# The ends of five stages of a two-layer decoder trunk: unit 18's second token half later, the last three products behind the next transposes

## The chip, the cores and the metric

The kernel runs on one core of a Trainium2 chip. The metric is the device time of one execution in microseconds (us). The core's engines work from queues of their own and meet only at semaphores: TensorE (PE in the rows, its weight loads PEld), VectorE (DVE), ScalarE (ACT), GpSimd (POOL) and SyncE (SP), which issues most of the DMAs.

## What is computed

256 tokens of 1024 channels go through two layers. Each is a SwiGLU block, a token mixer and a second SwiGLU block, every one of them followed by a residual sum and a layer norm. The mixer is a causal pooling in the first layer and attention over a window of 128 in the second.

```python
def post_norm(x, sub, g, b):
    return layer_norm(DEEPNORM_ALPHA * x + sub, g, b)

def swiglu(x, w_gate, w_up, w_down):
    h = jax.nn.silu(x @ w_gate) * (x @ w_up)
    return h @ w_down

# in each layer
x = post_norm(x, 0.5 * swiglu(x, ffn_w_gate[i, 0], ffn_w_up[i, 0], ffn_w_down[i, 0]), ln_g[i, 0], ln_b[i, 0])
x = post_norm(x, mix, ln_g[i, 1], ln_b[i, 1])
x = post_norm(x, 0.5 * swiglu(x, ffn_w_gate[i, 1], ffn_w_up[i, 1], ffn_w_down[i, 1]), ln_g[i, 2], ln_b[i, 2])
```

The feed-forward width is 2816, in 22 units of 128. All is float32 in and out.

## The kernel before

**Numbers.** A product is made in a reduced float format (fp32r) from split operands: high part times high part, high times low, low times high. `three` issues these as three matmuls. ScalarE makes the high part of a weight (L545 for gate and up weights `g_hi`, L553 for down weights `d_hi`), VectorE the low part (L847 `g_lo`, L851 `d_lo`); one half unit of gate-up weights per stage is left to GpSimd (L384).

**Stages.** There are four feed-forward stages, f = 0 to 3. Pooling stands between 0 and 1, attention between 2 and 3. A stage has units u = 0 to 21. `gate_up(f, u)` computes gate and up of a unit. ScalarE applies silu (L562), VectorE multiplies (L862, `h_of`), ScalarE takes the high part (L572, `h_hi_of`), VectorE the low part (L867, `h_lo_of`). `ffn_down(f, u, ts, hs)` adds the unit to the output sums in PSUM, which are four banks: token half t = 0, 1 and channel half h = 0, 1. Each bank and unit costs one `three` of 512 columns. The waits for a unit's data stand at its products for t = 0.

**The end of a stage on TensorE.** After `gate_up(21)`, which is L1209 to L1211 with 256 columns, come 39 matmuls of 512 columns: unit 19, t 0, h 1 (3); unit 18, t 1 (6); units 20 and 21, t 0, h 0 and then h 1 (12); units 19, 20 and 21, t 1, h 0 and then h 1 (18). Then the next stage begins: `transposes(e, 0)` (L1311) brings the normed tokens of half 0 to channel-major form, four tiles for each of two channel halves q, `gate_up_tokens(f, 0)` (L1244, L1245, L1249) multiplies them with units 0 and 1, and `transposes(e, 1)` takes token half 1.

**The layer norm** is VectorE's. For t = 0 and then 1 it does residual sum and statistics for both channel halves (L929, L935), L939, L940, centring (L947) and scaling (L960). The power -0.5 is GpSimd's (L451). L929 waits for the semaphore `acc_done`, which the last product into each bank raises. The transposes wait for L960. ScalarE copies what they give (L624), and the token products wait for that copy.

**Splits for the next stage.** `g_split(f, u)` on ScalarE and VectorE makes high and low parts of a unit's gate-up weights, in two halves. On ScalarE the first half waits for the weights' DMA and for a count in `g_used`, which TensorE raises after the last product of a unit's gate and up:

```python
                    else:
                        after(act, g_used, G0[f] + (-1, 0, 0, 2)[u] if u < 4 else G - 1 + 4 * it)
```

`G0[f]` is the number of units ahead of stage f; for the attention's weights, f = None, the same table has 0 for u = 1 on top of `G_QKV`, the number of units ahead of attention. `silu_of(f, 21)` waits for `g_used` at `G0[f] + 22`. `next_first(f, 1)` is unit 1 of what follows stage f. Its first half is VectorE's, its second GpSimd's, for f = 1 and 2.

## Time and profile before

| | |
|---|---|
| median of 3 runs | 866.58 us (865.11 to 866.79) |
| the profiled execution, its own time | 865.43 us |
| its span, first to last instruction | 863.6 us |
| granted TensorE clock, mean | 0.997 |
| TensorE busy | 841.8 us, 97% of the span |
| VectorE busy | 566.5 us |
| ScalarE busy | 419.1 us |

A matmul's row shows its whole passage, and the next starts before it ends. So what one costs in a row of many is the distance between starts: 39 matmuls between 389.23 and the start of the transposes at 398.11 stand 0.227 us apart. The profiled execution's own time is 1.8 us longer than its span, for what lies around it.

### The profile page before, as it was taken

The page shows a single profiled execution, that of the slowest core. Times are in us where ns is not written, and L with a number is a line of the kernel's source. Part 1 is how long each engine was busy: PE and PEld are TensorE (multiplying, and loading weights), DVE is VectorE, ACT ScalarE, POOL GpSimd, SP SyncE. Part 2 cuts the span into 40 slices and gives each one's busy share as a digit, 9 for nine tenths or more (in the row PEclk, how much of TensorE's full clock was granted, in tenths as well). Part 3 has the DMA queues.
Part 4 walks back from the last instruction along what each step waited for, and adds up shares of the span by engine and source line. Part 5 has one row for each costly group of instructions (what it writes and reads, how often), then busy time and mean ns, then how long its engine had stood idle before and what let it go on. Part 6 is the DMA issues. An engine that isn't in the chain of part 4 may idle for free.

```text
span 863.6 us, 12144 instructions
## 1 busy us (share of the span) xinstructions
PE 841.8 (97%) x4484; PEld 712.5 (83%) x4484; DVE 566.5 (66%) x775; ACT 419.1 (49%) x651; POOL 51.3 (6%) x61
## 2 busy tenths in 40 slices
PE   7999999999999999999999999999998999999995
PEld 6888888878888888887888888887765888888885
DVE  2785565669846565668666565679889855655656
ACT  2555454552535455454445454454665544554540
POOL 0050000024000000002000000010002000000000
PEclk9999999999999999999999999999999999999998
DMA  9997556292755655556556546453517575465501
GB/s 280 348 327 248 167 186 201 92 292 91 249 192 188 200 189 194 173 184 222 201 167 222 178 163 220 173 192 122 171 33 250 184 240 188 155 226 168 188 0 49
DMA packets 116142, 162.17 MB, mean 188 GB/s; under 512 B 3936, under 2 KB 97632, under 8 KB 116112
## 3 DMA queue, kind: packets, MB, share of 16 engines
q1 hardware_dynamic: 112656, 152.06, 52.9%
q0 software_dynamic: 2496, 9.44, 3.2%
q8 instruction: 19, 0.31, 0.1%
q10 hardware_dynamic: 960, 0.27, 0.1%
q14 instruction: 11, 0.09, 0.0%
HBM read 160.70 MB, written 1.05 MB: 187 GB/s over the span
## 4 chain that ended last, share of the span: by engine, by line
PE 93%; DVE 4%; issue 1%; ACT 1%; DMA 1%; DVEq 0%; POOL 0%; SPq 0%
PE ps L1278 28%; PE ps L1276 16%; PE ps L1209 10%; PE ps L1210 10%; PE ps L1211 10%; PE ps L1275 4%; PE ps L1244 1%; PE ps L1245 1%; PE ps L1249 1%; PE ps L1229 1%; PE ps L1074 1%; PE ps L1077 1%; PE ps L1083 1%; PE ps L1311 1%; PE ps L1039 1%
## 5 line engine op out<-in xcount | busy, mean ns | idle before, releaser
L1278 PE MATMUL ps<-xT,g_hi 128*128 128x512 f32 x1064 | 379.3, 396 | 0.0
L1276 PE MATMUL ps<-xT,g_lo 128*128 128x256 f32 x1216 | 314.1, 279 | 0.0
L1276 PEld LDWEIGHTS ps<-xT,g_lo 128*128 128x128 f32 x1216 | 229.1, 188 | 12.5
L847 DVE TENSOR_TENSOR g_lo<-raw_g,g_hi 128x1024 fp32r<-128x1024 f32 x178 | 221.6, 1249 | 24.1 <-ACT g_hi L545 24.1
L1278 PEld LDWEIGHTS ps<-xT,g_hi 128*128 128x128 f32 x1064 | 199.7, 188 | 41.2
L857 DVE TENSOR_TENSOR gu<-ps,gu 128x512 f32<-128x512 f32 x76 | 52.5, 691 | 221.7 <-ACT gu L568 221.7
L545 ACT ACTIVATE g_hi<-raw_g 128x1024 fp32r<-128x1024 f32 x184 | 192.0, 1052 | 4.5 <-DMA raw_g<-in_ffn_w_up 2.9
L568 ACT ACTIVATE gu<-ps 128x512 f32<-128x512 f32 x76 | 45.6, 600 | 273.9 <-PE ps L1278 273.9
L1209 PE MATMUL ps<-d_hi,hT_hi 128*128 128x512 f32 x352 | 137.6, 391 | 2.1 <-DVE hT_lo L867 2.1
L1210 PE MATMUL ps<-d_lo,hT_hi 128*128 128x512 f32 x352 | 137.0, 389 | 0.0
L1211 PE MATMUL ps<-d_hi,hT_lo 128*128 128x512 f32 x352 | 136.9, 389 | 0.0
L851 DVE TENSOR_TENSOR d_lo<-raw_d,d_hi 128x1024 fp32r<-128x1024 f32 x96 | 117.3, 1224 | 5.0 <-ACT d_hi L553 5.0
L553 ACT ACTIVATE d_hi<-raw_d 128x1024 fp32r<-128x1024 f32 x96 | 99.9, 1047 | 3.1 <-DMA raw_d<-in_ffn_w_down 3.1
L1211 PEld LDWEIGHTS ps<-d_hi,hT_lo 128*128 128x128 f32 x352 | 66.1, 188 | 14.2
L1210 PEld LDWEIGHTS ps<-d_lo,hT_hi 128*128 128x128 f32 x352 | 66.1, 188 | 14.0
L1209 PEld LDWEIGHTS ps<-d_hi,hT_hi 128*128 128x128 f32 x352 | 66.1, 188 | 13.1 <-DVE hT_lo L867 2.4
L1275 PE MATMUL ps<-xT,g_hi 128*128 128x512 f32 x152 | 60.3, 396 | 0.0
L572 ACT ACTIVATE hT_hi<-hf_sink 128x256 fp32r<-128x256 f32 x82 | 34.3, 418 | 34.2 <-DVE hf_sink L862 33.8
L867 DVE TENSOR_TENSOR hT_lo<-hf_sink,hT_hi 128x256 fp32r<-128x256 f32 x82 | 36.5, 445 | 3.4 <-ACT hT_hi L572 3.4
L384 POOL TENSOR_TENSOR g_lo<-raw_g,g_hi 128x1024 fp32r<-128x1024 f32 x6 | 14.4, 2392 | 376.3 <-DVE g_lo L847 374.5
L562 ACT ACTIVATE gu<-gu 128x256 f32<-128x256 f32 x76 | 30.9, 407 | 5.7 <-DVE gu L857 5.7
L862 DVE TENSOR_TENSOR hf_sink<-gu 128x256 f32<-128x256 f32 x76 | 32.6, 429 | 1.0 <-ACT gu L562 1.0
(154 smaller groups left out, 684.6 us busy)
## 6 DMA issues: line engine op xcount, KB each, us to landing
raw_d<-in_ffn_w_down SPq DMA_DIRECT2D x87, 512.0 KB, 4.0
raw_g<-in_ffn_w_gate SPq DMA_DIRECT2D x43, 1024.0 KB, 5.5
raw_g<-in_ffn_w_up SPq DMA_DIRECT2D x43, 1024.0 KB, 7.9
raw_g<-in_attn_w_qkv SPq DMA_DIRECT2D x6, 1024.0 KB, 6.6
raw_d<-in_attn_w_o SPq DMA_DIRECT2D x8, 512.0 KB, 3.8
gb<-in_ln_g POOLq DMA_DIRECT2D x5, 512.0 KB, 4.0
gb<-in_ln_b POOLq DMA_DIRECT2D x4, 512.0 KB, 6.0
xn<-in_x SPq DMA_DIRECT2D x2, 512.0 KB, 6.1
```

The lines of the kernel that those rows point to most:

```text
L545: act.activation(g_half(g_hi, g_slot(f, u), half), src(G, half), ACT.Copy).then_inc(g_hi_done, 1)
L553: act.activation(d_hi[:, E % D_SLOTS, :], raw_d[:, (E // 2) % 2, E % 2, :], ACT.Copy).then_inc(d_hi_done, 1)
L568: act.activation(gu[:, u % 2, :, :], both[:, :, S:2 * S], ACT.Copy).then_inc(low_done, 1)
L847: dve.tensor_tensor(g_half(g_lo, g_slot(f, u), half), src(G, half), g_half(g_hi, g_slot(f, u), half).bitcast(f32), ALU.subtract).then_inc( ...
L851: dve.tensor_tensor(d_lo[:, E % D_SLOTS, :], raw_d[:, (E // 2) % 2, E % 2, :], d_hi[:, E % D_SLOTS, :].bitcast(f32), ALU.subtract).then_in ...
L857: dve.tensor_tensor(gu[:, u % 2, :, :], both[:, :, 0:S], gu[:, u % 2, :, :], ALU.add).then_inc(gu_done, 1)
L1209: pe.matmul(out_, l_hi, r_hi, start=start, stop=False)
L1210: pe.matmul(out_, l_hi, r_lo, start=False, stop=False)
L1211: return pe.matmul(out_, l_lo, r_hi, start=False, stop=stop)
L1275: pe.matmul(bank, w_hi, xT[:, k, :, :], start=True, stop=False)
L1276: last = pe.matmul(bank[:, S:2 * S], w_lo, xT_hi[:, k, :], start=False, stop=False)
L1278: last = pe.matmul(bank, w_hi, xT[:, k, :, :], start=False, stop=k == KT - 1)
```

## The change

In every stage, unit 18's two groups for t = 1 leave their place between unit 19 and unit 20 and are issued with the rest of t = 1. The last product of a stage, unit 21 into the bank t 1, h 1 (three matmuls), becomes `last_down`. It is issued behind `transposes(e, 0)` of what follows the stage; after stage 0 it stands behind the first `means` of pooling, and after stage 3 it stays at the end. The last product of attention's output, `wo` unit 7 into t 1, h 1, also goes behind the next transposes. A count that the transposes raised (`d_used`) is raised by a later matmul.

On ScalarE and VectorE the first half of `next_first(f, 1)`, for f = 1 and 2, is made at the end of unit 20 and no longer at the end of unit 21.

```diff
@@ ScalarE, unit(f, u)
                 if f == 0 and u == UNITS - 2:
                     g_split(1, 0)
+                if f in (1, 2) and u == UNITS - 2:
+                    g_split(*next_first(f, 1), halves=(0,))
                 if f < 3 and u == UNITS - 1:
-                    g_split(*next_first(f, 1))
+                    g_split(*next_first(f, 1), halves=(0, 1)[f > 0:])
@@ VectorE, unit(f, u)
-                if u == UNITS - 1:
-                    if f == 0:
-                        g_split(1, 0, halves=(1,))
-                    elif f < 3:
-                        g_split(*next_first(f, 1), halves=(0,))
+                if f == 0 and u == UNITS - 1:
+                    g_split(1, 0, halves=(1,))
+                elif f in (1, 2) and u == UNITS - 2:
+                    g_split(*next_first(f, 1), halves=(0,))
@@ TensorE, pooling
-                    if t == 0 and k == 0:
+                    if t == 1 and src == 0 and k == 0:
                         ins.then_inc(d_used, 1)
@@
             means(0, 0, 0, True, True)
+            last_down(0)
             means(1, 0, P, True, False)
@@ TensorE, attention
             transposes(e, 0)
+            last_down(2)
             qkv(0, 0, 0, part=0, d_counted=True)
@@
             for h in range(2):
-                for k in range(5, 8):
+                for k in range(5, 8 - h):
                     wo(k, (1,), hs=(h,))
@@ TensorE, gate_up_tokens
-                    pe.matmul(out_, xT_hi[:, k, tok], w_hi[:, :, :, k, :], start=k == 0, stop=False)
+                    ins = pe.matmul(out_, xT_hi[:, k, tok], w_hi[:, :, :, k, :], start=k == 0, stop=False)
+                    if f > 1 and t == 0 and k == 0:
+                        ins.then_inc(d_used, 1)
@@ TensorE, the stages
+            def last_down(f):
+                ffn_down(f, UNITS - 1, (1,), hs=(1,))
+
@@
-                transposes(e, 0, used=(0, 2, 1, 1)[f])
+                transposes(e, 0, used=(0, 2, 0, 0)[f])
+                if f == 2:
+                    last_down(1)
+                elif f == 3:
+                    down(D_WO + 7, xT_hi[:, 7, :], xT_lo[:, 7, :], (1,), False, True, hs=(1,))
@@
                 ffn_down(f, last_u + 1, (0,), hs=(1,))
-                ffn_down(f, last_u, (1,))
                 for h in range(2):
                     for u in (last_u + 2, last_u + 3):
                         ffn_down(f, u, (0,), hs=(h,))
                 for h in range(2):
-                    for u in range(last_u + 1, UNITS):
+                    for u in range(last_u, UNITS - h):
                         ffn_down(f, u, (1,), hs=(h,))
                 if f == 0:
-                    pool_pe(pe)
+                    pool_pe(pe, last_down)
                 if f == 2:
-                    attention_pe(pe, three, down, transposes)
+                    attention_pe(pe, three, down, transposes, last_down)
+                if f == 3:
+                    last_down(f)
```

Here `last_u` is 18. ScalarE at the end of stage 1, before: unit 20's last two instructions, unit 21 (silu and high part) and the two halves of the split for the next stage.

```order
L572 ACTIVATE hT_hi<-hf_sink 128x256 [waits hf_done]
L553 ACTIVATE d_hi<-raw_d 128x1024 [waits d_used,d_in0]
L562 ACTIVATE gu<-ps 128x256 [waits g_used]
L572 ACTIVATE hT_hi<-hf_sink 128x256 [waits hf_done]
L545 ACTIVATE g_hi<-raw_g 128x1024 [waits g_used,g_in0]
L545 ACTIVATE g_hi<-raw_g 128x1024
```

The same place after:

```order
L572 ACTIVATE hT_hi<-hf_sink 128x256 [waits hf_done]
L553 ACTIVATE d_hi<-raw_d 128x1024 [waits d_used,d_in0]
L545 ACTIVATE g_hi<-raw_g 128x1024 [waits g_used,g_in0]
L562 ACTIVATE gu<-ps 128x256 [waits g_used]
L572 ACTIVATE hT_hi<-hf_sink 128x256 [waits hf_done]
L545 ACTIVATE g_hi<-raw_g 128x1024
```

The first half's copy, with its wait for `g_used`, has moved from behind unit 21 to ahead of unit 21's silu.

VectorE at the same place, before: unit 20's low parts, unit 21's product and low part, the split's first half, the layer norm.

```order
L867 TENSOR_TENSOR hT_lo<-hf_sink,hT_hi 128x256 [waits h_hi_done]
L851 TENSOR_TENSOR d_lo<-raw_d,d_hi 128x1024 [waits d_hi_done]
L862 TENSOR_TENSOR hf_sink<-gu,ps 128x256 [waits silu_done]
L867 TENSOR_TENSOR hT_lo<-hf_sink,hT_hi 128x256 [waits h_hi_done]
L847 TENSOR_TENSOR g_lo<-raw_g,g_hi 128x1024 [waits g_hi_done]
L929 SCALAR_TENSOR_TENSOR xn<-ps,xn 128x512 [waits acc_done]
```

After (lines moved by one or two):

```order
L869 TENSOR_TENSOR hT_lo<-hf_sink,hT_hi 128x256 [waits h_hi_done]
L853 TENSOR_TENSOR d_lo<-raw_d,d_hi 128x1024 [waits d_hi_done]
L849 TENSOR_TENSOR g_lo<-raw_g,g_hi 128x1024 [waits g_hi_done]
L864 TENSOR_TENSOR hf_sink<-gu,ps 128x256 [waits silu_done]
L869 TENSOR_TENSOR hT_lo<-hf_sink,hT_hi 128x256 [waits h_hi_done]
L930 SCALAR_TENSOR_TENSOR xn<-ps,xn 128x512 [waits acc_done]
```

The split's low half now stands ahead of unit 21's product. TensorE behind stage 1, after: the transposes, `last_down(1)` and the first token products; before, L1311's rows were followed by L1244 at once.

```order
L1319 MATMUL ps<-cst,xn 128x128 [waits xn_done]
L1319 MATMUL ps<-cst,xn 128x128 x3
L1212 MATMUL ps<-d_hi,hT_hi 128x512
L1213 MATMUL ps<-d_lo,hT_hi 128x512
L1214 MATMUL ps<-d_hi,hT_lo 128x512
L1247 MATMUL ps<-g_hi,xT 128x512 [waits x_hi_done,g_lo_done]
L1250 MATMUL ps<-g_lo,xT 128x512
```

The three matmuls have come in between the transposes and the products that wait for ScalarE's copy.

## Rows read from the trace of the kernel before

**Rows 1.** The page, part 1: busy time, share, instructions of TensorE.
```profile
PE   841.8 (97%) x4484; PEld 712.5 (83%) x4484; DVE 566.5 (66%) x775; ACT 419.1 (49%) x651; POOL 51.3 (6%) x61
```
**Rows 2.** Timeline, ScalarE, end of stage 1: start, duration, line, operation, idle before.
```profile
389.43 0.38 ACT L562 ACTIVATE gu<-ps 128x256 f32<-128x256 f32 x1 [1.89 <-PE ps L1211]
...
390.63 1.99 ACT L545 ACTIVATE g_hi<-raw_g 128x1024 fp32r<-128x1024 f32 x2
```
**Rows 3.** Timeline, VectorE, end of stage 1.
```profile
389.85 0.42 DVE L862 TENSOR_TENSOR hf_sink<-gu,ps 128x256 f32<-128x256 f32 x1 [1.05 <-ACT gu L562]
390.75 0.42 DVE L867 TENSOR_TENSOR hT_lo<-hf_sink,hT_hi 128x256 fp32r<-128x256 f32 x1 [0.48 <-ACT hT_hi L572]
391.70 1.23 DVE L847 TENSOR_TENSOR g_lo<-raw_g,g_hi 128x1024 fp32r<-128x1024 f32 x1 [0.53 <-ACT g_hi L545]
392.86 0.69 DVE L929 SCALAR_TENSOR_TENSOR xn<-ps,xn 128x512 f32<-128x512 f32 x1
...
397.31 1.41 DVE L960 SCALAR_TENSOR_TENSOR xn<-xn,rstd,gb 128x512 f32<-128x512 f32 x2
...
399.96 0.67 DVE L929 SCALAR_TENSOR_TENSOR xn<-ps,xn 128x512 f32<-128x512 f32 x1
```
**Rows 4.** Timeline, TensorE, end of stage 1 and entry of stage 2.
```profile
389.23 0.40 PE L1209 MATMUL ps<-d_hi,hT_hi 128*128 128x512 f32 x1
...
397.87 0.39 PE L1211 MATMUL ps<-d_hi,hT_lo 128*128 128x512 f32 x1
398.11 1.32 PE L1311 MATMUL ps<-cst,xn 128*128 128x128 f32 x8
399.55 0.47 PE L1244 MATMUL ps<-g_hi,xT 128*128 128x512 f32 x1
...
406.40 0.50 PE L1244 MATMUL ps<-g_hi,xT 128*128 128x512 f32 x1
```
**Rows 5.** Timeline, TensorE, a wait in stage 0 and the matmuls behind it.
```profile
184.08 0.50 PE L1209 MATMUL ps<-d_hi,hT_hi 128*128 128x512 f32 x1 [2.12 <-DVE hT_lo L867]
184.42 0.40 PE L1210 MATMUL ps<-d_lo,hT_hi 128*128 128x512 f32 x1
```
**Rows 6.** Timeline, end of stage 0: that product, unit 21's low part, pooling's first matmuls.
```profile
190.63 0.40 PE L1209 MATMUL ps<-d_hi,hT_hi 128*128 128x512 f32 x1
...
192.15 0.42 DVE L867 TENSOR_TENSOR hT_lo<-hf_sink,hT_hi 128x256 fp32r<-128x256 f32 x1 [0.48 <-ACT hT_hi L572]
...
199.60 3.81 PE L1025 MATMUL ps<-qT,xn 128*128 128x128 f32 x32
```
**Rows 7.** Timeline, attention's end and entry of stage 3, TensorE.
```profile
668.62 1.32 PE L1311 MATMUL ps<-cst,xn 128*128 128x128 f32 x8 [1.99 <-DVE xn L960]
670.05 0.47 PE L1244 MATMUL ps<-g_hi,xT 128*128 128x512 f32 x1
```
**Rows 8.** Timeline, end of stage 3, TensorE and VectorE.
```profile
845.94 0.40 PE L1209 MATMUL ps<-d_hi,hT_hi 128*128 128x512 f32 x1
...
847.46 0.42 DVE L867 TENSOR_TENSOR hT_lo<-hf_sink,hT_hi 128x256 fp32r<-128x256 f32 x1 [0.48 <-ACT hT_hi L572]
...
849.57 0.69 DVE L929 SCALAR_TENSOR_TENSOR xn<-ps,xn 128x512 f32<-128x512 f32 x1 [1.68 <-PE ps L1211]
...
856.67 0.67 DVE L929 SCALAR_TENSOR_TENSOR xn<-ps,xn 128x512 f32<-128x512 f32 x1
```
**Rows 9.** Timeline, GpSimd and VectorE splits: one beside GpSimd in stage 0; GpSimd's in stage 1.
```profile
178.04 5.70 POOL L427 TENSOR_TENSOR raw_d<-raw_d,q_sb 128x1024 f32<-128x1024 f32 x2 [115.86 <-DMA raw_d<-in_pool_w]
178.10 3.44 DVE L847 TENSOR_TENSOR g_lo<-raw_g,g_hi 128x1024 fp32r<-128x1024 f32 x1
...
393.09 2.39 POOL L384 TENSOR_TENSOR g_lo<-raw_g,g_hi 128x1024 fp32r<-128x1024 f32 x1 [173.72 <-DVE g_lo L847]
```
**Rows 10.** Windows: stretch, length, busy times, PEclk (the granted clock), DMA share, GB/s.
```profile
180.00:190.00 10.00, 7.88 (x57) 7.21 (x57) 8.51 (x8) 4.28 (x6) 3.74 (x2) 1.00 1.03 325
...
855.00:863.60 8.60, 0.00 (x0) 0.00 (x0) 6.01 (x11) 0.00 (x0) 0.99 (x1) 0.74 0.33 122
```

More of the change, by code:

```diff
@@ L1015, in _, with pool_pe @@
                     layer_norm(5)
-        def pool_pe(pe):
+        def pool_pe(pe, last_down):
             def means(t, src, columns, first, last):
@@ L1050, in pool_pe, with attention_pe @@
             maps(1)
-        def attention_pe(pe, three, down, transposes):
+        def attention_pe(pe, three, down, transposes, last_down):
             ident = cst[:, 0, :]
```

## The prediction

> **What bounds the kernel now.** Read the engines' busy shares first: TensorE works in 97% of the span [rows 1]. So a matmul that is only moved costs and saves nothing by itself. What counts is the time in which TensorE has nothing to start, and the tail behind its last product, where VectorE's layer norm sets the end. Then read the timeline at each stage's end, by the distance between starts. From 389.23 to 398.11 stand 39 matmuls [rows 4]: 0.2275 us each, without a gap. Then come eight transposes. A pass of 128 columns takes 0.114 us (32 in 3.81 us, less 0.16 for the last one's passage) [rows 6], so eight are 0.91 us, but the token product starts 1.44 us behind the first of them [rows 4]. The missing 0.53 us are the second channel half's wait for VectorE and the token product's wait for ScalarE's copy. The first matmul behind a wait costs 0.11 us more than its place in a row: 0.34 us to the next start, from 184.08 to 184.42 [rows 5].
>
> Next, the norm at the end of stage 1. Unit 21's low part is finished at 390.75 + 0.42 = 391.17, 1.94 us behind 389.23, where `gate_up(21)` has ended for TensorE [rows 3, 4]. Stage 3 has 847.88 - 845.94 = 1.94 and stage 0 has 192.57 - 190.63 = 1.94 [rows 6, 8]. It is the bare chain of silu, product, high part and low part, the same at four stage ends. TensorE comes to unit 21 after 12 matmuls, 2.73 us, so 0.79 us of cover are left. That number decides what follows.
>
> **Unit 18 moved: all four stages.** Six matmuls go from ahead of unit 21 to behind it. TensorE comes there 1.36 us sooner, 1.37 us after `gate_up(21)`, and the chain needs 1.94. So unit 21's first product waits 0.58 us, 0.6 with the semaphore, plus 0.11 for the first matmul: a new stall of 0.7 us. The sums of token half 0, and with them the norm, come 2.73 - 1.94 - 0.15 = 0.65 us sooner.
>
> **Stage 3, the tail.** Its norm is not waited for by TensorE but is the end of the kernel. The first L929 goes from 849.57 to 848.9. The last bank is due at VectorE's fourth sum, at 856.67 before [rows 8] and 856.0 then. TensorE is done with it at 845.94 + 39 x 0.2275 + 0.16 + 0.7 = 855.7, still in time by 0.3 us. Gain: 0.65 us.
>
> **Stage 0.** Here the splits are not moved. The stall is +0.7. TensorE then waits for nothing else: pooling's first matmul stood at 199.60 [rows 6], 0.1 us behind the last product's slot. That 0.1 goes. The three last products move behind the first means and delay nothing but the second sums of the norm, which pooling needs only after its maps of token half 0. Cost: 0.6 us.
>
> **Stages 1 and 2, the split moved.** The wait it brings along is for `g_used` at G0[f+1] + 0, which is the count that TensorE raises behind `gate_up(21)` itself, the same that unit 21's silu waits for. ScalarE did sit idle 1.89 us ahead of that silu [rows 2], room for a copy, but the wait keeps it from using the room. The copy starts at 389.43 where the silu did. Queued behind it are the silu and everything of unit 21, and TensorE waits for these. A copy is 1.05 us in its queue (two in 1.99, overlapping by 0.1) [rows 2]. VectorE's low half starts at 390.52, takes 1.22 to 1.23 [rows 3], and stands ahead of `h_of(21)`, which starts at 391.66 and no longer at 389.85 [rows 3]: 1.81 us late. The low part of unit 21 ends at 392.98. TensorE came to it at 390.60 and waits until 393.02: 2.42 us, and 0.11 for the first matmul, 2.53 in all. Thirty matmuls remain ahead of the transposes (39 less 6 less 3): 393.13 + 6.82 = 399.95. VectorE's norm, 1.15 us later than before (L929 goes from 392.86 to 394.0, and the first half of L960 from 398.01 to 399.2) [rows 3], is ahead of that. So the transposes run without a wait to 400.86, the three last products fill to 401.54, and the token product starts there: 1.99 us after its old 399.55 [rows 4]. The copy that it needs is done at 401.1, hidden.
>
> The second sum of token half 1 now needs that last product: about 401.7, where VectorE took it up at 399.96 [rows 3], +1.75. TensorE is 1.99 - 0.11 later, so the norm of half 1 stays in step, and a remaining 0.1 us at the second transposes closes. Per stage +1.8 us at 406.40 [rows 4]. The end of stage 2 has the same pattern (39 matmuls, the same chain, the same transposes), so two times 1.8, 3.6 us. The half split itself is done earlier, and GpSimd's half (2.39 us) [rows 9] begins 0.5 us later, both off the path. The loads that SyncE issues behind it belong to units 4 and up, later in the stage.
>
> **The attention's last product moved.** TensorE waits there for the norm, 1.99 us [rows 7]. Three matmuls taken from before the wait only lengthen it, and put behind the transposes they take 0.68 us, of which the copy's wait hides 0.32 (the second four transposes start with the second half of L960, 0.66 us behind the first, and are done 1.11 us behind 668.62; the product starts 1.43 behind it [rows 7]) and the first-matmul cost another 0.11. Cost: 0.25 us. The idle there grows to 2.7 us.
>
> **Sum.** 0.6 + 1.8 + 1.8 + 0.25 - 0.65 = +3.8 us, on the profiled execution 865.43 + 3.8 = 869.2. The median of the runs is 866.58, 1.15 above it, so the forecast for a median is 870.4 us, slower by 0.44%. The terms' own bounds: each of the five stage-end costs may be off by 0.2 to 0.4 us (what a wait hides of the three matmuls), which makes +2.6 to +5.0.
>
> **A rule weighed.** VectorE's split took 3.44 us beside GpSimd's 5.70 us, and 1.23 elsewhere [rows 3, 9], so the two engines hold each other up. GpSimd's half split of stage 1 moves to about 393.6 to 396.0, and the centring L947, which reads two operands from SBUF, to 397.1: 1.1 us clear of it. The Trainium skill ("SBUF — State Buffer", "SBUF: two separate sides") says that the port pair of GpSimd and VectorE is an exclusive lock for a whole instruction, taken by a VectorE instruction with two SBUF inputs. By that rule an overlap would cost the rest of GpSimd's instruction, and none is expected here; the trace's 3.44 us agrees with a blocking, and no row tells how long a centring would be held.
>
> **Rivals.**
> (a) The wait is met early: some count makes `g_used` reach the value before `gate_up(21)` ends. Then copy and low half run in the idle 1.89 us, unit 21 is on time, and stages 1 and 2 pay what stage 0 pays, 0.7, less 0.53 and 0.1 of filled waits: +0.1 each. Sum 0.6 + 0.2 + 0.25 - 0.65 = +0.4, 867.0 us. For it speaks only the idle; against it stand the table and the place where TensorE raises the count. Chance 0.08.
> (b) Faster: unit 21 doesn't hold TensorE at all. It decides where the chain behind `gate_up(21)` falls from 1.94 to under 1.37 us. Then the moves only fill waits: stage 0 gains 0.1, stages 1 and 2 0.6 each, the tail 1.36, attention loses 0.25: -2.4, 864.2 us. Against it: 1.94 us at every stage end with ScalarE and VectorE idle before it, and the split added to it at two. Chance 0.03.
> (c) The granted clock falls in a new stall. It stayed at 1.00 through the wait of 2.12 us, and was 0.74 on average over the 8.6 us behind the last matmul [rows 5, 10], so it does fall in idleness. The new stalls of 2.4 and 2.7 us are a little longer than any that the trace shows clean. At 1.2 GHz for 2.4 each matmul of the 30 that follow would cost 0.23 us more, up to 6.8 us a stage: 873 to 884 us. Chance 0.03.
> (d) The norm of stages 1 and 2 runs into GpSimd's half split after all and is held up to 2.4 us; TensorE has 0.75 us of slack there (399.95 against 399.2), so up to +1.6 a stage, 872 to 873.6 us. Chance 0.03.
>
> **How the numbers follow.** The forecast has the remaining chance, 0.83. Its range, +2.6 to +5.0 on 866.58 and 0.7 us for how medians of one kernel scatter (865.11 to 866.79 in three runs), is 868.5 to 872.3; I take 868.2 to 872.2, which leaves out (a), (b), (c), most of (d) and little else, under 2 in 10. What a measurement can tell from no change is about 0.2%, 1.7 us. Slower by more: the forecast, (c) and (d), less 0.03 for a sum that comes out too small: 0.86. Within: (a) and that 0.03, with a rounding 0.11. Faster: (b), 0.03.
>
> **What would show it.** In the changed trace, ScalarE's g_hi copy starts right behind `gate_up(21)` at the ends of stages 1 and 2, and its silu 1 us later. TensorE has two waits of about 2.4 us for hT_lo there, and two of 0.6 us at the ends of stages 0 and 3. The transposes of stages 2 and attention show no wait for L960, attention's end one of 2.7 us. The tail behind the last matmul gets shorter by 1.3 us, from 8.6 to about 7.3. If the copy runs before the end of `gate_up(21)`, (a) holds and the time stays near 867. If the waits are there and the time isn't, the span is set by something that I read as hidden.

## The result and the profile after

The changed kernel takes 871.97 us at the median of 8 runs (868.88 to 873.95). The kernel before, run beside it, takes 865.36 us (864.78 to 866.79, 8 runs). The ratio is 1.007, with a 95% interval of 1.0056 to 1.0085: slower, by 6.6 us. The time lies inside the predicted range, 1.6 us above the forecast. Part of that is luck: the range was laid on a median of 866.58 us from three runs, and the same kernel's eight runs have 865.36. As a difference, +6.6 us lies above the forecast of +3.8 and its bounds of +2.6 to +5.0. The profiled execution took 870.46 us, +5.0 on the one of before.

The page's part 1, of after, answers to [rows 1]:

```profile
PE   842.6 (97%) x4484; PEld 714.9 (82%) x4484; DVE 566.9 (65%) x775; ACT 418.6 (48%) x651; POOL 51.5 (6%) x61
```

The work is the same: as many matmuls, 0.8 us more of passage. So the time lies in gaps. The waits of TensorE (us in total, times, longest us) name them:

```profile
PE ps L1212 <- DVE hT_lo L869: 6.9, 4, 2.3
...
PE ps L1319 <- DVE xn L961: 2.7, 1, 2.7
```

Before, the trace had one wait for hT_lo, 2.12 us, in stage 0 [rows 5], and one of 1.99 us for xn [rows 7]. Now there are four for hT_lo, one at each stage's end, and xn's has grown.

The end of stage 1 of after, in the timeline of ScalarE and VectorE, answers to [rows 2, 3]:

```profile
389.56 1.06 ACT L545 ACTIVATE g_hi<-raw_g 128x1024 fp32r<-128x1024 f32 x1 [1.95 <-PE ps L1214]
390.53 0.36 ACT L562 ACTIVATE gu<-ps 128x256 f32<-128x256 f32 x1
...
390.66 1.23 DVE L849 TENSOR_TENSOR g_lo<-raw_g,g_hi 128x1024 fp32r<-128x1024 f32 x1 [1.79 <-ACT g_hi L545]
391.80 0.41 DVE L864 TENSOR_TENSOR hf_sink<-gu,ps 128x256 f32<-128x256 f32 x1
...
392.69 0.43 DVE L869 TENSOR_TENSOR hT_lo<-hf_sink,hT_hi 128x256 fp32r<-128x256 f32 x1 [0.48 <-ACT hT_hi L572]
```

ScalarE's copy waits 1.95 us for TensorE and starts when `gate_up(21)` has ended. The silu stands behind it, and VectorE's low half of the split stands ahead of unit 21's product. TensorE in the same place, against [rows 4]:

```profile
389.30 0.40 PE L1212 MATMUL ps<-d_hi,hT_hi 128*128 128x512 f32 x1
...
393.17 0.50 PE L1212 MATMUL ps<-d_hi,hT_hi 128*128 128x512 f32 x1 [2.32 <-DVE hT_lo L869]
393.51 0.39 PE L1213 MATMUL ps<-d_lo,hT_hi 128*128 128x512 f32 x1
...
400.11 1.03 PE L1319 MATMUL ps<-cst,xn 128*128 128x128 f32 x8
400.90 0.47 PE L1212 MATMUL ps<-d_hi,hT_hi 128*128 128x512 f32 x1
...
408.41 0.50 PE L1247 MATMUL ps<-g_hi,xT 128*128 128x512 f32 x1
```

Unit 21's first product starts 3.87 us behind 389.30, after a wait of 2.32. The transposes have no wait, the last products follow them, and the second group of token products starts at 408.41, 2.01 us later than at 406.40.

Attention's end and the start of stage 3, of after, against [rows 7]:

```profile
672.55 1.97 PE L1319 MATMUL ps<-cst,xn 128*128 128x128 f32 x8 [2.67 <-DVE xn L961]
674.17 0.78 PE L1212 MATMUL ps<-d_hi,xT 128*128 128x512 f32 x1
674.74 0.63 PE L1213 MATMUL ps<-d_lo,xT 128*128 128x512 f32 x1
```

These rows are long. The last product's second matmul starts 0.57 us behind its first; in stage 1 the same step, from 400.90 to 401.22, took 0.32. The windows (length, busy us of PE, PEld, DVE, ACT and POOL with their counts, granted clock, DMA share, GB/s) say why:

```profile
670.00:675.00 5.00, 2.45 (x10) 2.36 (x11) 4.45 (x6) 1.04 (x2) 1.59 (x2) 0.73 0.62 198
675.00:680.00 5.00, 5.00 (x22) 4.03 (x22) 4.06 (x8) 2.05 (x3) 0.55 (x1) 0.93 0.71 225
```

The granted clock falls behind the wait of 2.67 us. The loss is (0.27 + 0.07) x 5 = 1.7 us of the full rate of 2.4 GHz, for a stretch of twice that at 1.2 GHz. Below this is called a low stretch; rival (c) named it.

The end of stage 3, of after, against [rows 8]:

```profile
851.74 0.38 ACT L562 ACTIVATE gu<-ps 128x256 f32<-128x256 f32 x1 [2.81 <-PE ps L1214]
...
853.54 0.50 PE L1212 MATMUL ps<-d_hi,hT_hi 128*128 128x512 f32 x1 [0.45 <-DVE hT_lo L869]
...
854.54 0.69 DVE L930 SCALAR_TENSOR_TENSOR xn<-ps,xn 128x512 f32<-128x512 f32 x1 [1.06 <-PE ps L1214]
...
860.92 0.39 PE L1214 MATMUL ps<-d_hi,hT_lo 128*128 128x512 f32 x1
```

Unit 21 waits 0.45 us. VectorE's idle ahead of its first residual sum has shrunk from 1.68 to 1.06 us. What each term of the sum measured is told behind the experiments.

### The profile page after: what moved, and what is told of

It reads as the page before. It is cut to its first block, busy times and chain, and to the rows that moved or that the text cites. A ratio compares the mean times of both kernels' runs of the same rounds, so it can differ in the third digit from the quotient of the medians.

```text
span 868.6 us, 12144 instructions
## 1 busy us (share of the span) xinstructions
PE 842.6 (97%) x4484; PEld 714.9 (82%) x4484; DVE 566.9 (65%) x775; ACT 418.6 (48%) x651; POOL 51.5 (6%) x61
## 4 chain that ended last, share of the span: by engine, by line
PE 91%; DVE 5%; ACT 2%; issue 1%; DMA 1%; DVEq 0%; POOL 0%; SPq 0%; ACTq 0%
PE ps L1283 28%; PE ps L1281 16%; PE ps L1212 10%; PE ps L1214 10%; PE ps L1213 10%; PE ps L1280 4%; PE ps L1247 1%; PE ps L1250 1%; PE ps L1254 1%; PE ps L1232 1%; PE ps L1076 1%; PE ps L1079 1%; PE ps L1085 1%; PE ps L1319 1%; DVE d_lo L853 1%
## 5 line engine op out<-in xcount | busy, mean ns | idle before, releaser
L853 DVE TENSOR_TENSOR d_lo<-raw_d,d_hi 128x1024 fp32r<-128x1024 f32 x96 | 119.5, 1247 | 5.2 <-ACT d_hi L553 5.2
```

Of the source, the lines that this page charges most:

```text
L853: dve.tensor_tensor(d_lo[:, E % D_SLOTS, :], raw_d[:, (E // 2) % 2, E % 2, :], d_hi[:, E % D_SLOTS, :].bitcast(f32), ALU.subtract).then_in ...
```

## The experiments

Two theories had to be told apart. **The wait theory** is the forecast's: what the change costs is the stall at unit 21, most of it because the moved copy waits for `g_used`. **The clock theory** is rival (c) in a small size: the new and longer waits let the granted clock fall in a part of the runs, and that explains the rest of the median and the spread of 5 us where the kernel before had 2. A third question was whether the parts are worth something without the faults. Each ratio below is against the kernel before, run beside the kernel on the same chip. Runs' mean clocks are given where they bear on it; they include the tail, in which TensorE has no work, so that 0.997 or more is a run without a low stretch. The fourteen profiled executions of this document bear that out: windows of 5 us show no low stretch in the six with 0.997 or more, one in the four with 0.995 or 0.996 (after, e6, e8, e9), two in the three with 0.993 or 0.994 (e1, e4, e5) and three in the one with 0.992 (e3), each a loss of 1.7 us of full rate.

### The split back (e1)

```diff
@@ after, ScalarE (and VectorE likewise)
-                if f in (1, 2) and u == UNITS - 2:
-                    g_split(*next_first(f, 1), halves=(0,))
                 if f < 3 and u == UNITS - 1:
-                    g_split(*next_first(f, 1), halves=(0, 1)[f > 0:])
+                    g_split(*next_first(f, 1))
```

> The changed kernel with one part undone: ScalarE and VectorE make the first half of the next stage's split at the end of unit 21 again; TensorE's order is the changed one. Theory (the split's wait for g_used costs 1.8 us at each of stages 1 and 2): +0.4 us over the kernel before, and TensorE's wait for hT_lo at those two ends is 0.6 us and not 2.3. Rival (TensorE's new order is what costs): the time stays near the changed kernel's, +4 us or more. Second theory (a stretch of about 3.4 us at 1.2 GHz, 1.7 us lost, follows the long idle ahead of stage 3, as in the profiled run of the changed kernel): up to +2.1 us where a run has it, since that idle of 2.7 us is still there.

Measured: 867.05 us, ratio 1.0016 (1.0007 to 1.0025, 11 runs). Without the split's move 1.5 of the 6.6 us are left. The eleven runs fall into two groups: 866.00 to 866.45 at a mean clock of 0.997 (five runs), and 867.98 to 868.55 at 0.993 to 0.996 (five), with one run between. So two things are at work, and the split is the larger. The profiled execution, 868.33 us, has two low stretches, behind a wait of 1.78 us in stage 0 and one of 2.67 us behind attention.

### The wait asked for earlier (e2)

The split stays where the change puts it, and its count in `g_used` is one that TensorE has long reached.

```diff
-                        after(act, g_used, G_QKV + (-1, 0, 0, 1, 3, 4)[u])
+                        after(act, g_used, G_QKV + (-1, -20, 0, 1, 3, 4)[u])
...
-                        after(act, g_used, G0[f] + (-1, 0, 0, 2)[u] if u < 4 else G - 1 + 4 * it)
+                        after(act, g_used, G0[f] + (-1, -20 if f < 3 else 0, 0, 2)[u] if u < 4 else G - 1 + 4 * it)
```

> The changed kernel with one number changed: the moved split waits for g_used at the value that unit 1 of the stage raises (the last reader of its slot), 20 lower, so the copy can run while gate_up(21) does. Theory (it was the wait and not the place): as the kernel with the split put back, +0.4 us over before, silu of unit 21 right behind gate_up(21), TensorE's wait for hT_lo 0.6 us at all four ends. Rival (two more instructions ahead of unit 21 cost by their work): +1.8 to +3.6 us. The clock stretch ahead of stage 3 may add 1.7 us in a run.

Measured: 867.16 us, ratio 1.0012 (1.0003 to 1.0021, 11 runs). Timeline of e2, end of stage 1:

```profile
388.03 1.04 ACT L545 ACTIVATE g_hi<-raw_g 128x1024 fp32r<-128x1024 f32 x1
390.03 0.38 ACT L562 ACTIVATE gu<-ps 128x256 f32<-128x256 f32 x1 [0.95 <-PE ps L1214]
...
391.83 0.50 PE L1212 MATMUL ps<-d_hi,hT_hi 128*128 128x512 f32 x1 [0.45 <-DVE hT_lo L869]
```

The copy now runs in ScalarE's idle time ahead of the silu, which is rival (a) made true by hand. Unit 21's wait is 0.45 us where it was 2.32. The instruction's place was harmless; the count that it waits for did the harm.

### The split alone (e4)

The kernel before with the split's move and nothing else.

```diff
@@ before, ScalarE (and VectorE likewise)
+                if f in (1, 2) and u == UNITS - 2:
+                    g_split(*next_first(f, 1), halves=(0,))
                 if f < 3 and u == UNITS - 1:
-                    g_split(*next_first(f, 1))
+                    g_split(*next_first(f, 1), halves=(0, 1)[f > 0:])
```

> The kernel before with only the split moved on ScalarE and VectorE (wait unchanged); TensorE's order is that of before. Theory: unit 21 is ready at 3.75 us behind gate_up(21) and TensorE comes to it at 2.73, so it waits 1.0 us, and the norm and all behind it come 1.1 us later at each of two stages: +2.2 us. Rival (the split's place is harmless while unit 18 stands ahead as cover): within 0.3 us of before.

Measured: 867.99 us, ratio 1.0020 (1.0011 to 1.0029, 11 runs), +2.4. Timeline of e4:

```profile
393.82 0.50 PE L1210 MATMUL ps<-d_hi,hT_hi 128*128 128x512 f32 x1 [0.96 <-DVE hT_lo L869]
```

With unit 18 still ahead of it TensorE has the 0.79 us of cover that the prediction counted, and waits 0.96 instead of 2.32. The split's move harms by itself, and unit 18's makes it worse by just the six matmuls (2.32 - 0.96 = 1.36 us). The wait is what the theory said. The median of +2.4 isn't free of the clock, though: the profiled execution, 869.97 us, has two low stretches, and the three runs at 0.997 or 0.998 took 865.59, 866.82 and 868.06.

### Attention's last product back (e3)

```diff
@@ after, attention and entry of stage 3
-                for k in range(5, 8 - h):
+                for k in range(5, 8):
...
-                elif f == 3:
-                    down(D_WO + 7, xT_hi[:, 7, :], xT_lo[:, 7, :], (1,), False, True, hs=(1,))
```

> The changed kernel with attention's last product put back ahead of the transposes; all else as changed. Arithmetic without a clock: 0.25 us less than the changed kernel, +3.5 over before, idle ahead of stage 3 2.0 us. Theory (the idle of 2.7 us there is what lets the clock fall): 1.5 to 2 us less than the changed kernel, and mean clock 0.997 as before. Rival (the waits of 2.3 us at the ends of stages 1 and 2 let it fall as well): the difference to the changed kernel stays under 1 us and runs at 0.993 to 0.995 remain.

Measured: 872.78 us, ratio 1.0073 (1.0059 to 1.0087, 5 runs), not below after. The clock theory in its first form said that the wait of 2.7 us behind attention is what lets the clock fall. It is 2.0 us here, and the low stretches are still there. Windows of e3:

```profile
185.00:190.00 5.00, 5.00 (x32) 5.00 (x32) 3.21 (x4) 3.66 (x5) 0.00 (x0) 0.71 0.87 271
...
585.00:590.00 5.00, 5.00 (x19) 4.03 (x18) 4.25 (x8) 0.00 (x0) 1.43 (x2) 0.77 0.62 200
...
675.00:680.00 5.00, 4.69 (x17) 3.72 (x18) 4.86 (x10) 3.09 (x4) 0.55 (x1) 0.66 1.03 340
```

And the waits of e3's TensorE, in its timeline:

```profile
183.27 0.50 PE L1212 MATMUL ps<-d_hi,hT_hi 128*128 128x512 f32 x1 [2.12 <-DVE hT_lo L869]
...
394.39 0.50 PE L1212 MATMUL ps<-d_hi,hT_hi 128*128 128x512 f32 x1 [2.32 <-DVE hT_lo L869]
...
582.52 0.50 PE L1212 MATMUL ps<-d_hi,hT_hi 128*128 128x512 f32 x1 [2.32 <-DVE hT_lo L869]
...
675.30 1.10 PE L1319 MATMUL ps<-cst,xn 128*128 128x128 f32 x5 [2.01 <-DVE xn L961]
```

Four waits of 2.0 to 2.3 us, and a low stretch behind three of them: behind 183.27, 582.52 and 675.30, not behind 394.39. The wait at 183.27 is the same 2.12 us behind which the clock stayed at 1.00 in the kernel before [rows 5, 10]. So waits of about 2 us let the clock fall at some times and not at others, and the first form of the theory is gone.

### Unit 18 alone (e5), the last products alone (e6)

```diff
@@ e5: before
-                ffn_down(f, last_u, (1,))
...
-                    for u in range(last_u + 1, UNITS):
+                    for u in range(last_u, UNITS):
@@ e6: before, stages 1 and 2 alone
-                    for u in range(last_u + 1, UNITS):
+                    for u in range(last_u + 1, UNITS - h * (f in (1, 2))):
```

e6 has `last_down(1)` and `last_down(2)` behind `transposes(e, 0)`, as the change has them.

> The kernel before with only unit 18's t = 1 products (six matmuls) issued with the rest of t = 1, in all four stages; last products, split and attention as before. Theory: unit 21 is reached 1.37 us behind gate_up(21) and ready at 1.94, so 0.7 us of stall at each of four stage ends; the norm comes 0.65 us sooner, which stages 0 to 2 can't use in full; the tail gives back 0.65. Stage 0 +0.6, stages 1 and 2 +0.3 to +0.5 each, stage 3 -0.65: +0.6 to +1.0 us. Rival (TensorE is free to start the norm sooner and the stage follows it): -0.6 us at each end, -2.5 us.

> The kernel before with only the last product of stages 1 and 2 issued behind the next transposes. Theory: the norm is ready at 398.06 in the time of the trace before, TensorE comes to the transposes at 397.43 and waits; then transposes and three matmuls end 1.8 us later, at 399.85 in place of 399.55: +0.2 us a stage, +0.4 in all. Rival (the three matmuls fill the copy's wait at no cost): 0 or -0.2 us a stage.

Measured: e5 867.26 us, ratio 1.0020 (1.0005 to 1.0034, 9 runs); e6 867.11 us, ratio 1.0016 (1.0004 to 1.0028, 9 runs). Neither part gains anything alone. Timeline of e5, then of e6:

```profile
392.87 0.50 PE L1209 MATMUL ps<-d_hi,hT_hi 128*128 128x512 f32 x1 [0.45 <-DVE hT_lo L867]
```

```profile
397.75 1.32 PE L1317 MATMUL ps<-cst,xn 128*128 128x128 f32 x8 [0.53 <-DVE xn L960]
```

e5 shows the stall of unit 21 without the split: 0.45 us. e6 shows the other side of the trade: products taken from ahead of the transposes leave TensorE waiting 0.53 us for the norm, which is not earlier. Both came out above what was expected (+1.8 where +0.6 to +1.0 was, +1.7 where +0.4 was). The profiled execution of e5 has low stretches in two places, and e6's nine runs reach from 864.76 at 0.998 to 869.21 at 0.994.

### Half of unit 18 (e7)

The cover is 0.79 us, that is three matmuls of 0.2275 us and not six. So one of the two groups is moved, together with the last products of stages 1 and 2; the split, attention's product and the last products of stages 0 and 3 stay where they were.

```diff
@@ before
-                ffn_down(f, last_u, (1,))
+                ffn_down(f, last_u, (1,), hs=(0,))
...
-                    for u in range(last_u + 1, UNITS):
+                    for u in range(last_u + 1 - h, UNITS - h * (f in (1, 2))):
```

`last_down(1)` and `last_down(2)` stand behind `transposes(e, 0)`, as in e6.

> The kernel before with one channel half of unit 18's t = 1 product (three matmuls) moved behind, in all four stages, and the last product behind the transposes in stages 1 and 2; attention, pooling and the split as before. Theory: three matmuls of cover are kept, so TensorE reaches unit 21 at 2.05 us against 1.94, without a stall; the norm comes 0.68 us sooner; the tail gives 0.68 us, stages 1 and 2 0.3 us each, stage 0 0.1 us: -1.4 us, 0.16% faster. Rival (any shift of unit 18 costs): no gain, or slower.

Measured: 864.37 us, ratio 0.9993 (0.9982 to 1.0004, 11 runs), 1.1 us under the kernel before by the medians, which the interval doesn't tell from none; 1.4 were expected. Six of the runs lie at 864.13 to 864.37. Timeline of e7:

```profile
396.94 1.32 PE L1317 MATMUL ps<-cst,xn 128*128 128x128 f32 x8 [0.40 <-DVE xn L960]
```

There is no wait for hT_lo left at the ends of stages 1 to 3, the cover being just used up. At the end of stage 0 this execution waits 1.10 us; the account of stage 0 below comes back to it.

### GpSimd's scaling later (e8)

The wait of 2.12 us in stage 0 [rows 5] was blamed on VectorE's split being held up beside GpSimd's scaling [rows 9]. Here the scaling is put off to unit 20 of stage 0.

```diff
@@ before, GpSimd, ahead of the two scalings (L427)
+            gp.wait_ge(h_lo_done, UNITS - 2)
```

> The kernel before with GpSimd's scaling of the pooling weights (two instructions, 5.7 us, in stage 0) held until VectorE has made unit 19's low part. Theory (VectorE's split and that low part were blocked by GpSimd, and TensorE's wait of 2.1 us in stage 0 comes from it alone): the wait goes, -2.2 us, and fewer runs with a clock stretch at 1.2 GHz behind it. Rival (the blocking only moves to unit 20's or 21's chain): 0 to +2 us, a wait for hT_lo of 1 to 3 us at the end of stage 0.

Measured: 864.61 us, ratio 0.9984 (0.9974 to 0.9994, 10 runs). The wait for hT_lo is gone, but only 0.8 of the expected 2.2 us came. Timeline of e8, attention's end, in which the rest went:

```profile
659.59 5.47 POOL L384 TENSOR_TENSOR g_lo<-raw_g,g_hi 128x1024 fp32r<-128x1024 f32 x2 [18.74 <-DVE g_lo L848]
...
662.08 3.52 DVE L948 SCALAR_TENSOR_TENSOR xn<-xn,mv,gb 128x512 f32<-128x512 f32 x2
...
666.92 1.32 PE L1312 MATMUL ps<-cst,xn 128*128 128x128 f32 x8 [2.81 <-DVE xn L961]
```

The kernel before had it much the same there, in rows that the prediction had not read:

```profile
661.75 4.93 POOL L384 TENSOR_TENSOR g_lo<-raw_g,g_hi 128x1024 fp32r<-128x1024 f32 x2 [18.39 <-DVE g_lo L847]
...
664.60 3.30 DVE L947 SCALAR_TENSOR_TENSOR xn<-xn,mv,gb 128x512 f32<-128x512 f32 x2
```

Two centrings beside GpSimd's split take 3.52 us in e8 and took 3.30 before; two scalings of the same shape take 1.41 [rows 3], and so do two centrings at the end of stage 1 of after, where GpSimd's split is over (397.32 in its timeline). In e8 GpSimd's power stands behind its split as well, so that the scaling waits another 0.51 us for it (it starts at 666.12, behind GpSimd's L452). TensorE, which came 2.2 us earlier, waits 2.81 us for the norm and no longer 1.99: 0.8 of the 2.2 us are given back. The windows of e8 show the clock low behind this wait:

```profile
660.00:670.00 10.00, 7.07 (x31) 5.29 (x30) 9.31 (x13) 2.32 (x4) 5.88 (x3) 0.91 0.38 121
670.00:680.00 10.00, 9.75 (x43) 7.88 (x43) 7.67 (x14) 4.13 (x6) 1.68 (x3) 0.92 0.60 200
```

(0.09 + 0.08) x 10 = 1.7 us of full rate, the same as in after. Nine of the ten runs of e8 have a clock of 0.995 or 0.996.

### The waits filled (e10), beside the changed kernel again (e11)

The decisive pair for the clock theory. e10 is the changed kernel with extra matmuls of 512 columns whose results are not read, in front of the places where it waits: 9 in stage 0, 10 ahead of unit 21's products in stages 1 and 2, and 11 ahead of the transposes behind attention. In stage 0 they stand ahead of unit 19's first product, behind a wait for unit 19's own product on VectorE (`hf_done`), which keeps them in the place of the stall; that part of the edit isn't shown. e11 is the changed kernel as it is, on the same chip.

```diff
@@ after
+            def fill(bank, n, weights, moving):
+                for i in range(n):
+                    pe.matmul(ps[:, bank, :], weights, moving, start=True, stop=True)
...
+                if f == 3:
+                    fill(WORK, 11, xT_hi[:, 7, 0:P], d_hi[:, (D_WO + 7) % D_SLOTS, 0:512])
                 transposes(e, 0, used=(0, 2, 0, 0)[f])
...
                     for u in (last_u + 2, last_u + 3):
+                        if f in (1, 2) and h == 0 and u == last_u + 3:
+                            fill_unit(f, last_u + 2, WORK, 10)
                         ffn_down(f, u, (0,), hs=(h,))
```

> The changed kernel, whole, with matmuls of 512 columns whose results nobody reads put into TensorE's long waits: 9 ahead of unit 19's product in stage 0 (2.0 us), 10 ahead of unit 21's in stages 1 and 2 (2.3 us each), 11 ahead of the transposes behind attention (2.5 us). They shorten no wait for data. Clock theory (idle waits of 1.8 to 2.7 us let the granted clock fall to 1.2 GHz for about 3.4 us in many runs, 1.7 us lost each time): the runs gather near the changed kernel's fastest, +3.6 us over before, about 2 to 3 us under its median, mean clock 0.997. Rival (the spread is something else, such as DMA): median and spread as the changed kernel's in the same job, or slower by what is filled in.

> The changed kernel as it is, beside the one with filled waits on the same chip. Both theories: +4 to +8 us over before, with most runs at a mean clock under 0.997.

Measured: e10 869.62 us, ratio 1.0058 (1.0044 to 1.0071, 5 runs, from 869.07 to 869.94); e11 871.97 us, ratio 1.0096 (1.0075 to 1.0117, 4 runs, 868.75 to 875.15). Timeline of e10:

```profile
390.66 2.43 PE L1313 MATMUL ps<-d_hi,hT_hi 128*128 128x512 f32 x10
393.14 0.50 PE L1212 MATMUL ps<-d_hi,hT_hi 128*128 128x512 f32 x1
```

The waiting is the same: unit 21 starts at 393.14 where it started at 393.17. Only, TensorE works through it. And now the kernel that has more work is 2.35 us faster than the one with less, and its runs lie within 0.9 us where the others reach over 6.4. The windows of e10 around attention's end:

```profile
665.00:675.00 10.00, 9.81 (x47) 7.71 (x47) 9.71 (x14) 3.08 (x5) 5.78 (x3) 1.00 0.33 108
675.00:685.00 10.00, 9.85 (x47) 7.95 (x46) 9.05 (x16) 4.71 (x7) 1.68 (x3) 1.00 0.63 210
```

The granted clock is 1.00 where it was 0.73 and 0.93. This shows that the spread, and 2.35 us of the +6.5 at which e11 stands, come from the clock in the waits. The four runs of e11 order themselves by it: 868.75 us at 0.997, 871.22 and 872.72 at 0.993, 875.15 at 0.990. The first of these is the profiled one. Its rows of waits for hT_lo and xn are those of after, to the 0.1 us. Its window behind attention's end, and two rows of its timeline:

```profile
670.00:680.00 10.00, 7.88 (x40) 6.38 (x41) 9.61 (x16) 3.46 (x5) 1.71 (x3) 1.00 0.68 211
```

```profile
672.12 1.32 PE L1319 MATMUL ps<-cst,xn 128*128 128x128 f32 x8 [2.67 <-DVE xn L961]
...
850.05 0.38 ACT L562 ACTIVATE gu<-ps 128x256 f32<-128x256 f32 x1 [2.81 <-PE ps L1214]
```

The same kernel, the same waits, no low stretch, and 1.71 us less than the profiled execution of after. Of these, 0.43 us were there before the low stretch (672.12 against 672.55). From the transposes to the silu of unit 21 in stage 3 e11 takes 177.93 us and after 179.19, so this low stretch cost 1.26 us of time. In the kernel before the same way is 177.52 us, and in e6, which has the same code there and a low stretch, 179.16: 1.64. So a low stretch is a loss of 1.7 us of full rate and cost 1.3 to 1.6 us of time.

### Half of unit 18 and the later scaling together (e9), and filled (e12)

e9 holds the edits of e7 and e8. e12 adds eight unread matmuls to it, ahead of the transposes behind attention.

```diff
@@ e9
+                if f == 3:
+                    for i in range(8):
+                        pe.matmul(ps[:, WORK, :], xT_hi[:, 7, 0:P], d_hi[:, (D_WO + 7) % D_SLOTS, 0:512], start=True, stop=True)
```

> The kernel before with both parts that gained alone: one channel half of unit 18 behind (and the last product behind the transposes in stages 1 and 2), and GpSimd's scaling of the pooling weights held until unit 19's low part. Theory: the gains add, -1.1 and -1.0 us in the medians alone, so -2 to -3.5 us. Rival (the norm that comes sooner in stage 0 meets GpSimd): no more than one of them alone.

> As e9_both, with 8 unread matmuls (1.8 us) ahead of the transposes behind attention, the one long wait that is left. Clock theory: the median falls by the share of runs that had a clock stretch there times 1.7 us, 0.3 to 1.7 us under e9_both, and mean clock 0.997 in nearly all runs. Rival: same median as e9_both.

Measured: e9 864.88 us, ratio 0.9991 (0.9980 to 1.0003, 11 runs); e12 863.84 us, ratio 0.9983 (0.9974 to 0.9992, 11 runs). The gains of e7 and e8 don't add up in e9. Its runs fall into four at 863.29 to 864.09 with a clock of 0.997 to 0.998, and seven at 864.65 to 865.56 with 0.995 or 0.996. Its one long wait is the 2.8 us behind attention. Windows of e9, and then of e12:

```profile
660.00:670.00 10.00, 7.09 (x32) 5.37 (x31) 9.31 (x13) 2.27 (x5) 6.30 (x3) 0.95 0.30 97
670.00:680.00 10.00, 9.75 (x42) 7.78 (x42) 7.61 (x14) 4.90 (x7) 1.67 (x3) 0.88 0.66 219
```

```profile
660.00:670.00 10.00, 8.85 (x42) 6.79 (x41) 9.28 (x14) 2.24 (x5) 6.33 (x3) 1.00 0.34 105
670.00:680.00 10.00, 9.96 (x47) 7.81 (x47) 9.21 (x15) 4.71 (x7) 1.68 (x3) 1.00 0.66 212
```

Eight unread matmuls remove the upper group: all eleven runs of e12 are at 0.997 or 0.998, between 862.95 and 864.21. It is the fastest kernel tried, 1.6 us under the kernel before, a small gain that the interval does tell from none, and 8.1 under the changed one (e11), all run beside each other.

## Why the prediction was right, and where it was not

**The stall at unit 21 (stages 1 and 2): right.** Forecast: the copy starts where the silu did, unit 21 waits 2.42 us, +1.8 us per stage at the second group of token products. Measured: 2.32 us and +2.01 at 408.41. The start of stage 1 was already 0.06 late, so the stage costs 1.95. Stage 2 repeats it: attention's second transposes start at 595.41 in after and at 591.34 before, +4.07 in sum. e2 shows that the count in `g_used` is the cause. Rival (a) is what e2 built, and its price held: the two runs of e2 at 0.997 are 865.94 and 865.95, +0.4 on the median of 865.59 beside it, as (a) had it for the whole kernel. The Trainium skill ("Perfetto Trace Analysis", "Tensor Engine Instruction (MATMUL, LD_WEIGHTS)") says that ScalarE, VectorE and GpSimd keep strictly to their order; the rows agree, the silu began at 390.53 behind the copy, where before it had begun at 389.43.

**Stage 0: right in its mechanism, not in this profile's sum.** Forecast +0.6; the profiled execution of after enters stage 1 at +0.06. Its timeline shows GpSimd's scaling and VectorE beside it:

```profile
179.54 2.63 DVE L869 TENSOR_TENSOR hT_lo<-hf_sink,hT_hi 128x256 fp32r<-128x256 f32 x1
182.09 3.42 DVE L853 TENSOR_TENSOR d_lo<-raw_d,d_hi 128x1024 fp32r<-128x1024 f32 x1
...
192.11 0.50 PE L1212 MATMUL ps<-d_hi,hT_hi 128*128 128x512 f32 x1 [1.79 <-DVE hT_lo L869]
```

Before, GpSimd held up the split at 178.10 (3.44 us) [rows 9] and then the low part that TensorE was to wait for:

```profile
181.46 2.57 DVE L867 TENSOR_TENSOR hT_lo<-hf_sink,hT_hi 128x256 fp32r<-128x256 f32 x1
```

Now the split is through first, and held up are that low part, already at 179.54 (2.63 us for 0.42), and the instruction behind it (3.42). The wait of 2.12 us at 184.08 is gone. TensorE comes to the stage's end earlier while ScalarE doesn't: unit 21's silu stands behind two copies of ScalarE (188.33, 1.99 us) and starts at 190.23, 1.47 us behind the end of `gate_up(21)` at 188.76. So 1.79 us at unit 21 stand in the place of the old wait. Six matmuls less of cover are 1.36 of them; e7, with three less, waits 1.10 there in the same order of events. e3 has the code of after in stage 0 and shows the other order: 2.12 at 183.27, and 0.45 at unit 21. So two timings exist, and which one a run takes isn't decided by the change, as far as these runs show. The prediction had no term for this, because it took the wait at 184.08 for a fixed part of the kernel.

**Attention's end: right in size, wrong in what it set off.** The wait grew to 2.67 us (forecast 2.7). The last product put behind the transposes costs 0.41 us where 0.25 was forecast. From these transposes to the silu of unit 21 in stage 3 e11 takes 177.93 us at full clock, and the kernel before takes 177.52, from 668.62 [rows 7] to this row:

```profile
846.14 0.38 ACT L562 ACTIVATE gu<-ps 128x256 f32<-128x256 f32 x1 [2.80 <-PE ps L1211]
```

In the profiled execution of after, 1.67 us were added between the entry of the transposes (+3.93) and that silu (851.74, +5.60): this 0.41, and 1.26 for the low stretch, for which the sum had no term. This is the step that failed: rival (c) got a chance of 0.03, on the ground that the clock "stayed at 1.00 through the wait of 2.12 us". That was one execution. The kernel before has such stretches itself: of its 27 runs beside e1, five lie at 867.20 to 867.95 with clocks of 0.993 to 0.995, where the median is 865.59, and only six have a clock of 0.997. The price was wrong as well. 2.4 GHz came back soon enough that a low stretch cost 1.3 to 1.6 us, and not 6.8 us a stage.

**The tail: right.** Forecast -0.65. The silu stands 5.60 us later than before and the first residual sum 854.54 - 849.57 = 4.97: -0.63. The fourth sum, at 861.66, is due behind the last matmul at 860.92 + 0.39, so it is VectorE's chain that sets the end, as said. From 861.31, where the last matmul's passage ends, to the end of the span at 868.6 are 7.3 us, as forecast. Rival (b) stands where it was put: unit 21 holds TensorE at all four stage ends.

**Rival (d): not seen.** The norm of stage 1 runs free of GpSimd here (its split ends at 396.10, the centrings start at 397.32, and the transposes have no wait). But the prediction was wrong to say that no row tells how long a centring would be held: attention's end of the kernel before shows it, 3.30 us for two.

**The sum.** The two runs of the changed kernel at a clock of 0.997 took 868.88 and 868.75 us, +3.5 and +3.3 on the medians beside them; e10, with its waits filled, +4.2. Those medians hold low stretches of the kernel before too, but its 31 runs at 0.997 or 0.998, of the 80 beside the experiments, have a median of 865.31, so the comparison at equal clock comes out the same, +3.5. The forecast's arithmetic was +3.8, and it is borne out. The median's +6.6 has some 3 us more. By the count of low stretches above, the eight clocks, 0.992 to 0.997, make 1.5 of them a run, 2.0 to 2.4 us. The rest isn't accounted for; one run, 872.40 us at 0.995, is about 2 us longer than its clock explains. The forecast for the median was nevertheless only 1.6 us too low, because it started from 866.58 and not from 865.36: that is the luck in it.

**What stays open.** Which of several waits of about 2 us lets the clock fall in a given run, and why: e3 has three falls behind four nearly equal waits. And what decides between the two timings of stage 0. Of the 31 runs of the kernel before at full clock, eight lie at 863.42 to 863.92 us and the others at 864.89 to 865.72. The eight may be those without the 2.12 us wait. An estimate from the rows agrees: the kernel before would save 2.12 + 0.11 there and pay a wait of 1.79 - 1.36 = 0.43 and 0.11 at unit 21, which leaves 1.7 us. But no profile of such a run was taken.

## What to carry to other kernels

An instruction that is moved ahead takes its semaphore's count with it: ask what the count is for, and lower it to what the data need, before the queue behind it pays. Measure the cover in front of a waiting product (here 0.79 us) and move no more work from it than it holds: with three matmuls moved the kernel was no slower (0.9993, an interval that holds 1), with six it was. Where TensorE must wait some 2 us, matmuls whose results nobody reads can be cheaper than idleness, and one profile in which the clock stayed up is no proof that it does.

## What the runs showed of the hardware

- **The granted clock falls behind waits of 1.8 to 2.8 us, in some executions.** The fourteen profiled executions have 27 waits of TensorE from 1.78 to 2.81 us (those of the first 10 us and the tail aside), and a low stretch behind 13 of them; no low stretch stands elsewhere. Waits of 2.62 (e2) and 2.67 us (e11) left the clock at 1.00. In after it was 0.73 and 0.93 over 5 us each. One low stretch cost 1.3 to 1.6 us. Filled with matmuls, the same waits left it at 1.00 (e10, e12). The Trainium skill ("TensorE: Matmul & The Clock Gate", "Part 1: The HAM clock gate") says that the clock depends on how busy TensorE has been recently; the runs here agree, and add that equal waits don't end equally.
- **GpSimd and VectorE hold each other up.** A low part took 2.63 us for 0.42, a split 3.44 for 1.23, two centrings 3.52 for 1.41, and GpSimd's two half splits 5.47 where one alone took 2.39 [rows 9]. The Trainium skill ("SBUF — State Buffer", "SBUF: two separate sides") calls the port pair an exclusive lock held for a whole instruction, and the rows agree. What they add is that the instruction which is hit changes from run to run (after and e3 in stage 0), so that a stall of 2 us stands now here, now there.
